# Order of attention steps and value units: two block-attention steps beside each unit, one sparse-attention step ahead of the last unit

## The reference

```
q, k, v = split(h @ w_in, 3)           # 1024 -> 3 x 1024
s = q @ k.T * 64 ** -0.5, causal       # per head, 256 x 256
o = softmax(s) @ v
h = h + o @ w_out
```

## Time and profile before

| | us |
|---|---|
| median of 3 runs | 2950.37 |
| lowest, highest | 2949.48, 2950.72 |
| the profiled execution's own time | 2951.04 |
| its span in the trace | 2949.2 |
| TensorE busy in the span | 2826.3 (96%) |
| VectorE, ScalarE, GpSimd busy | 2083.9, 1457.5, 150.7 |

### The profile page before, as it was taken

The page is one execution under the profiler, slowest core; times in us unless marked ns, Lnnn a source line. Parts: engine busy times, 40 slices in busy tenths (PEclk is TensorE's granted clock), DMA queues, the critical chain, the costliest instruction groups (busy, mean ns, idle before and its releaser), DMA issues.

```text
span 2949.2 us, 53560 instructions
## 1 busy us (share of the span) xinstructions
PE 2826.3 (96%) x22724; PEld 2513.7 (85%) x22724; DVE 2083.9 (71%) x3259; ACT 1457.5 (49%) x1957; POOL 150.7 (5%) x257
## 2 busy tenths in 40 slices
PE   5999999999999999999999999999899999999998
PEld 5888899888888888998888878889788988887887
DVE  5986857668778868666776587754676677657774
ACT  2545644555445466445454365543554345436552
POOL 1000000200000000002000040000100000005000
PEclk9999999999999999999999999999999999999999
DMA  8775337538768753364475624554365556562452
GB/s 260 253 248 171 115 106 217 180 115 258 245 207 261 243 158 116 122 209 158 157 230 184 196 81 143 183 188 144 115 200 185 173 157 199 174 207 67 157 184 102
DMA packets 516702, 521.41 MB, mean 177 GB/s; under 512 B 16503, under 2 KB 513728, under 8 KB 516464
## 3 DMA queue, kind: packets, MB, share of 16 engines
q1 hardware_dynamic: 513856, 517.28, 54.8%
q0 software_dynamic: 816, 0.27, 0.1%
q10 hardware_dynamic: 1792, 0.44, 0.1%
HBM read 516.90 MB, written 1.05 MB: 176 GB/s over the span
## 4 chain that ended last, share of the span: by engine, by line
PE 83%; DVE 9%; ACT 5%; issue 2%; DMA 1%; POOL 0%; ACTq 0%; DVEq 0%; SPq 0%; POOLq 0%
PE P L65 81%; DVE wsp L74 3%; ACT wsp L71 2%; PE P L68 2%; DVE arena L82 1%; ACT arena L71 1%; DVE ACC L82 1%; DVE arena L74 1%; DVE X L74 1%; DMA raw<-in_nsa_w_in 1%; ACT HX L71 1%; ACT L71 0%; DVE HX L82 0%; DVE X L82 0%; DMA raw<-in_ada_w 0%
## 5 line engine op out<-in xcount | busy, mean ns | idle before, releaser
L65 PE MATMUL P<-HX,wsp 128*128 128x256 f32 (+1 forms) x10304 | 1610.2, 318 | 36.2 <-DVE wsp L74 13.9
L65 PEld LDWEIGHTS P<-HX,wsp 128*128 128x128 f32 x10304 | 1451.3, 192 | 174.8 <-issue 22.6
L74 DVE TENSOR_TENSOR wsp<-raw,wsp 128x2048 fp32r<-128x2048 f32 (+4 forms) x440 | 946.1, 2153 | 363.4 <-ACT wsp L71 362.9
L71 ACT ACTIVATE wsp<-raw 128x2048 fp32r<-128x2048 f32 (+4 forms) x440 | 791.1, 1800 | 541.9 <-PE P L65 470.1
L65 PE MATMUL P<-FG,wsp 128*128 128x256 f32 (+1 forms) x2816 | 496.1, 337 | 1.7 <-DVE wsp L74 1.7
L65 PEld LDWEIGHTS P<-FG,wsp 128*128 128x128 f32 x2816 | 428.5, 188 | 64.9 <-DVE wsp L74 2.9
L71 ACT ACTIVATE arena<-P 128x512 f32<-128x512 f32 (+3 forms) x384 | 215.0, 568 | 513.9 <-PE P L65 510.6
L74 DVE TENSOR_TENSOR arena<-arena,P 128x512 f32<-128x512 f32 (+2 forms) x232 | 151.0, 653 | 182.5 <-ACT arena L71 153.5
L65 PE MATMUL P<-arena 64*64 64x64 f32 (+9 forms) x4000 | 235.0, 259 | 9.7 <-DVE arena L74 3.4
L82 DVE SCALAR_TENSOR_TENSOR ACC<-raw,sm,ACC 128x256 f32<-128x256 f32 x476 | 230.8, 485 | 16.7
L65 PEld LDWEIGHTS P<-arena 64*64 64x64 f32 (+3 forms) x4000 | 185.7, 145 | 55.6 <-issue 29.8
(11 more groups left out here) (110 smaller groups left out, 1375.0 us busy)
## 6 DMA issues: line engine op xcount, KB each, us to landing
raw<-in_ffn_w SPq DMA_DIRECT2D x120, 1024.0 KB, 5.3
raw<-in_ada_w SPq DMA_DIRECT2D x72, 1024.0 KB, 5.1
raw<-in_w_in SPq DMA_DIRECT2D x52, 1024.0 KB, 5.2
raw<-in_ffn_w_gate SPq DMA_DIRECT2D x44, 1024.0 KB, 5.3
raw<-in_ffn_w_up SPq DMA_DIRECT2D x44, 1024.0 KB, 5.3
raw<-in_ffn_w_down SPq DMA_DIRECT2D x32, 1024.0 KB, 5.1
raw<-in_nsa_w_in SPq DMA_DIRECT2D x20, 1024.0 KB, 7.0
raw<-in_ffn_w SPq DMA_DIRECT2D x16, 768.0 KB, 4.4
```

What stands on the lines that cost most here:

```text
L65: return self if self.e is None else self.e.matmul(*a, skip_group_check=True, **k)
L71: return self if self.e is None else self.e.activation(*a, **k)
L74: return self if self.e is None else self.e.tensor_tensor(*a)
```

## The change

In block attention, step 0 is moved ahead of unit 8; behind unit 8 stand steps 1 and 2, behind unit 9 steps 3 and 4, behind unit 10 steps 5 and 6, behind unit 11 steps 7 to 10. On ScalarE step 0 comes behind the split of unit 11, as before, but ahead of the copy of unit 8's values. In sparse attention step 2 moves from behind the last unit of values to ahead of it. No arithmetic, buffer or transfer changes, and the splits keep their places among the steps.

```diff
+        STEPS = ((), (0,), (1, 2), tuple(range(3, 19)))
...
@@ nsa_pe, in the loop over x @@
-                if x >= 1:
-                    attend2_pe(e, 2 + 2 * j, jobs, 5120, [x - 1])
-            attend2_pe(e, 2 + 2 * j, jobs, 5120, range(3, 19))
+                attend2_pe(e, 2 + 2 * j, jobs, 5120, STEPS[x])
...
+        BEHIND = ((1, 2), (3, 4), (5, 6), (7, 8, 9, 10))
...
@@ moba_pe @@
+                if i == 8:
+                    attend2_pe(e, 3, moba_jobs(), 6144, [0])
                 b = take(e, ("mk", i))
...
                 if i >= 8:
-                    attend2_pe(e, 3, moba_jobs(), 6144, [i - 8])
-            attend2_pe(e, 3, moba_jobs(), 6144, range(4, 11))
+                    attend2_pe(e, 3, moba_jobs(), 6144, BEHIND[i - 8])
...
@@ moba_act @@
                 if i < 9:
                     ready_act(e, u)
+                if i == 8:
+                    attend2_act(e, 3, moba_jobs(), 6144, [0])
                 if i >= 8:
                     e.wait_ge(*MM.at(u))
...
-                    attend2_act(e, 3, moba_jobs(), 6144, [i - 8])
-            for i in range(4, 11):
-                attend2_act(e, 3, moba_jobs(), 6144, [i])
-                if i in LATER:
-                    ready_act(e, U["mk", 0][9 + LATER.index(i)])
+                    for s in BEHIND[i - 8]:
+                        attend2_act(e, 3, moba_jobs(), 6144, [s])
+                        if s in LATER:
+                            ready_act(e, U["mk", 0][9 + LATER.index(s)])
```

More of the change, by code:

```diff
@@ L2426, in nsa_act @@
                     e.activation(PTC, v3(P[bank["ptc", j]][:, :], 2), ACT.Copy).then_inc(*NAC.up((j, "ptc")))
[L2427 to L2430, removed]
-                if i in LATER:
-                    ready_act(e, U["kv", j][1 + LATER.index(i)])
+                for i in STEPS[x]:
+                    attend2_act(e, 2 + 2 * j, jobs, 5120, [i])
+                    if i in LATER:
+                        ready_act(e, U["kv", j][1 + LATER.index(i)])
         def nsa_dve(e, j, n):
@@ L2546, in nsa_dve @@
                         shares(t)
[L2547 to L2552, removed]
+                for i in STEPS[x]:
+                    attend2_dve(e, 2 + 2 * j, jobs, 5120, 0.125, [i])
+                    if i - 1 in LATER:
+                        ready_dve(e, U["kv", j][1 + LATER.index(i - 1)])
         MQ, MK, MV = ar(0, 8, 256), ar(2048, 8, 256), ar(4096, 2, 1024)
         LATER = (4, 6, 8)
+        BEHIND = ((1, 2), (3, 4), (5, 6), (7, 8, 9, 10))
         def moba_jobs():
@@ L2606, in moba_dve @@
                     ready_dve(e, u)
+                if i == 8:
+                    attend2_dve(e, 3, moba_jobs(), 6144, 0.125, [0])
                 if i >= 8:
[L2608 to L2612, removed]
+                    for s in BEHIND[i - 8]:
+                        attend2_dve(e, 3, moba_jobs(), 6144, 0.125, [s])
+                        if s - 1 in LATER:
+                            ready_dve(e, U["mk", 0][9 + LATER.index(s - 1)])
         Z = [ar(520 * i, 2, 260) for i in range(2)]
```

## The result

| | before | changed |
|---|---|---|
| median of 20 runs, us | 2950.27 | 2955.19 |
| lowest, highest | 2941.76, 2955.45 | 2948.28, 2957.77 |
| span of the profiled execution | 2949.2 | 2955.9 |

The ratio is 1.0015, 95% interval 1.0008 to 1.0021: slower by about 4.4 us, less than 0.2% and clear of the noise of 20 runs.

What follows compares the result with a forecast made beforehand. TensorE was taken to bound the kernel, with 83% of the chain that ended last. Block tail -0.2, clock +1.5 and sparse attention +1.5 gave +2.8 us, so 2953.2 us, range 2946 to 2957.

Steps and rivals of the forecast that it cites:

- The new wait behind unit 8: Block attention, between units 8 and 9: TensorE waits 5.7 us, in parts of 5.2 and 0.5, for scaled heads.
- What is given back in the tail: Block attention, behind unit 11: projection starts 0.2 us earlier, new wait included; range -0.8 to +1.5.
- The clock behind the wait: Block attention, unit 9: a lower clock after the new pause adds 1.5 us; bounds 0 and 2.8.
- Sparse attention: Both sparse parts: a wait before the last unit adds 0.75 us each, +1.5 in all; bounds 0 to 2.3 each.
- The sum: Whole kernel: -0.2 + 1.5 + 1.5 = +2.8 us, so 2953.2, expected too small to tell from no change.
- the faster ones: Block attention: no new wait, 2946.0 us, chance 0.08; also no wait for head 15, 2941.9, chance 0.03.
- the one with a late VectorE: Block attention behind unit 11: VectorE's lateness costs up to 5.3 us more, +8.1 in all, 2958.5; chance 0.08.
- The fourth: Low clock for all of unit 9, 2.8 instead of 1.5, and once in sparse attention: +5.6, 2956.0; chance 0.07.

Runs made afterwards that it cites:

- e3: Changed kernel with the split of unit 11 behind step 1 instead of ahead of step 0; block part 70.73 us, ratio to before 0.9990.
- e1: Kernel before with only the block attention order changed, sparse attention as before; block part 77.97 us, ratio to before 1.0006.
- e6: Changed kernel with the first two sparse projection splits behind step 2, under the last unit of values; sparse parts 58.99 and 58.98 us, ratio to before 0.9970.
- e2: Kernel before with only step 2 of sparse attention moved; sparse parts 65.52 and 65.55 us, ratio to before 1.0014.
- e4: Changed kernel with 41 unused matmuls filling the wait between units 8 and 9; block part 75.86 us, ratio to before 1.0015.
- e8: Kernel before, step order kept, with block attention's first two projection splits behind steps 1 and 2, under units 10 and 11; block 69.11 us, ratio 0.9983.
- e9: Sparse step order of before, first two sparse splits behind step 1; block steps as changed, splits under units; sparse parts 59.86 us, ratio to before 0.9948.
- e10: As e9, with the third sparse projection split behind steps 16 and 17 instead of 8 and 9; sparse parts 57.37 and 57.38 us, ratio to before 0.9936.
- e7: As e6, with block attention's splits also moved under units 8 to 11; block 67.58 us, sparse parts 58.98 us, ratio to before 0.9945.
- e11: As e7, with the third sparse projection split behind steps 16 and 17; sparse parts 56.32 and 56.33 us, ratio to before 0.9925.

## Why the prediction was right, and where its terms were off

- **The new wait behind unit 8**: forecast 5.2 and 0.5 us, released by GpSimd, because the split of unit 11 stands ahead of step 0. The trace has 5.32; e3 takes the split away and the wait shrinks to 0.69.
- **What is given back in the tail**: the forecast had VectorE's second split 3.99 us after unit 11's end; it is 4.00 (2084.57 to 2088.57). From there to the projection I carried over 6.99 us, and it took 5.49. The row I carried was taken at the lower clock (the values took 2.83 us then, 1.68 now). The projection was 0.7 shorter as well. But this is one draw: the same order took 6.17 in e1 and 6.95 in e6, where the low clock came back at that wait. (The upper bound that I gave for this term, +1.5, should have read +1.3, -0.2 and 1.5.)
- **The clock behind the wait**: forecast 1.5 from a unit of 7.47 us. The clock fell in the pause itself (0.95 in the stretch 2051 to 2053, with TensorE idle; the transposes start at 2053.38). The unit took 8.11, and the six transposes took 1.76, where I had 0.81 and a wait of 0.5. Unit 11 ended 44.88 us after the part's start instead of 42.56, so this term was 2.3; behind the same wait of 5.32 it was 1.9 in e1 (unit 7.73) and 1.0 in e6 (6.76). What is lost here is partly got back at the tail's wait, and the other way round: to the start of the projection the three took 54.37, 54.67 and 54.47. The part came out between 0.3 shorter and 0.8 longer than before, where I had 1.3 longer.
- **Sparse attention**: forecast +0.75 each. The wait is there as forecast (0.86), but the part is longer by 0.6 in one and by 1.7 in seven of the eight parts with the step moved and the splits in their old place (changed, e2, e3, e4). I priced the step's own wait, near enough, and took the tail for unchanged, though every part of the old order already had the clock at 0.50 behind its first split. With the step moved, the clock fell behind the third split too, for 1.1 us. This is the mis-sized term: 3.5 us measured in e2 against 1.5.
- **The sum**: +2.8 forecast; the ratio says +4.4 (2.4 to 6.2). Direction and mechanism held, and the closeness of the number owes something to luck: the block term was some 1 us too high and the sparse term 2 too low. I had also called the change too small to be told from none; 20 runs a side told it.
- **The rivals**: the faster ones did not occur, and the one with a late VectorE neither (VectorE waited 2.48 us for unit 11's end, against the 2.5 I had given it). The fourth, the low clock for longer behind unit 8 and once more in sparse attention, came true in part. Unit 9 stayed under the whole unit at 1.2 GHz that I had priced (8.11 against 8.7), and the extra low clock came in both sparse parts of e2, not in one, at the third split and not at the moved step. I had given it 0.07 because waits of 0.8 us fill little of the time; behind just such waits the clock fell. The measured +4.4 lies between my forecast and its +5.6.

## What to carry to other kernels

Before moving a step ahead, ask of each engine what stands in front of it in its own queue: here a 4.2 us preparation of later weights, harmless under a unit, became the path as soon as TensorE came back one unit sooner. Moving the preparations to where a long piece of TensorE work covers them made block attention's part 8.1 us of 77 shorter without moving a step (e8), and each sparse part 3.9 of 64 (e9), or 6.4 with the third one late (e10). With that done, the step order that had cost 0.15% was a gain of 1.5, 0.9 and 0.9 us in the three parts. When the whole differs by less than the unchanged stretches do from trace to trace, judge an edit by the length of its own stretch, in more than one trace, and by many runs of the whole.

## What had not been expected of the hardware

What a pause costs was not fixed by its length. In 13 traces TensorE paused 26 times for 3.3 to 3.6 us ahead of a unit like that of the earlier trace rows: 20 of these units took 7.46 to 7.49 us, four took 8.41 to 8.53 and two took 5.98 and 5.99, as if there had been no pause. Behind the same pause of 5.32 us unit 9 took 8.11, 7.73 and 6.76. In the changed kernel that pause had the granted clock at 0.95 in its last stretch and at 0.50 in the work behind it (2053 to 2059).

In sparse attention the clock fell with no pause over 0.86 us. Each part of the old order had one low spell, behind the first tail split. With step 2 moved, six of eight parts had it there and seven had one behind the third split. Where the first two splits stood under the unit (e6, e7, e9, e10, e11), there was none. And e4 shows that keeping the clock up at one wait does not keep it at the next.
